# A streaming encoder step on one core: norm sums of the FFN as columns, the adds of the second half on VectorE, a new order of transfers before the down projection, and three low parts on GpSimd

## What is computed

```python
x = x + mixed @ w_out                       # three kinds of attention heads
x = x + memory_attend(x, mem_k, mem_v, ...) # cross-attention to 256 memory tokens, ends in @ w_mem_o
u = rmsnorm(x, g_ffn) @ w_up                # D_FF = 2816, so 5632 columns
c = causal depthwise convolution of width 3 over tokens of u
a, b = split(c); x = x + (silu(a) * b) @ w_down
y = rmsnorm(x, g_final)
```

## Time and profile before

| | |
|---|---|
| median of 3 runs | 1693.22 us (1693.13 to 1694.28) |
| the profiled execution | 1690.41 us, its span from the first to the last instruction 1688.6 us |
| PE busy | 1627.8 us (96%) |
| PEld busy | 1500.7 us (89%) |
| DVE busy | 1180.0 us (70%) |
| ACT busy | 674.3 us (40%) |
| POOL busy | 489.6 us (29%) |
| mean granted TensorE clock | 0.99 of full speed |

### The profile page before, as it was taken

How to read it: one execution, slowest core, us unless ns; L and a number is a source line. 1 busy time by engine, 2 the same in 40 slices (tenths; PEclk the granted TensorE clock), 3 DMA queues, 4 the chain that set the end, 5 groups by cost and what they waited for, 6 DMA issues and landing times.

```text
span 1688.6 us, 29368 instructions
## 1 busy us (share of the span) xinstructions
PE 1627.8 (96%) x11113; PEld 1500.7 (89%) x11113; DVE 1180.0 (70%) x1595; ACT 674.3 (40%) x1283; POOL 489.6 (29%) x255
## 2 busy tenths in 40 slices
PE   9999999999999999999967999999999998999998
PEld 8999889776667799998967999999999988999987
DVE  7583587896667654446698888888888855766765
ACT  7320222686566531215335555555555531011022
POOL 2683132000000223430564323333332222333432
PEclk9999999999999999999979999999999999999999
DMA  5322220330213223316521221222222144123213
GB/s 209 103 75 82 82 61 16 114 95 1 113 51 98 85 94 123 108 38 268 186 92 35 69 69 62 78 78 78 78 78 77 39 175 167 59 100 106 78 63 113
DMA packets 71236, 155.93 MB, mean 92 GB/s; under 512 B 29680, under 2 KB 32976, under 8 KB 68336
## 3 DMA queue, kind: packets, MB, share of 16 engines
q1 hardware_dynamic: 68848, 145.33, 25.3%
q10 hardware_dynamic: 2304, 9.44, 1.6%
HBM read 119.61 MB, written 32.86 MB: 90 GB/s over the span
## 4 chain that ended last, share of the span: by engine, by line
PE 86%; DVE 7%; issue 3%; ACT 2%; POOL 1%; DMA 1%; SPq 0%; DVEq 0%; ACTq 0%; POOLq 0%
PE scores L2644 20%; PE scores L3356 19%; PE bank L2644 17%; PE bank L3356 8%; PE scores L2950 3%; PE bank L3010 3%; PE bank L3034 2%; PE scores L2740 2%; PE scores L2662 1%; DVE x L2387 1%; DVE kbuf L2177 1%; PE bank L3304 1%; PE bank L2653 1%; PE scores L2973 1%; PE bank L3068 1%
## 5 line engine op out<-in xcount | busy, mean ns | idle before, releaser
L3356 PE MATMUL scores<-c,up_w 128*128 128x288 f32 x2464 | 365.7, 298 | 10.6 <-ACT kept_a L1735 3.7
L3356 PEld LDWEIGHTS scores<-c,up_w 128*128 128x128 f32 x2464 | 344.4, 190 | 13.0 <-issue 9.8
L1115 POOL TENSOR_TENSOR w_hi<-w_raw,zero 128x1024 fp32r<-128x1024 f32 x34 | 67.8, 1994 | 582.9 <-DVE prob L2193 262.2
L2644 PE MATMUL bank<-s_hi,w_down 128*128 128x384 f32 (+2 forms) x476 | 133.1, 339 | 8.2 <-POOL w_down L1253 5.5
L2644 PE MATMUL scores<-s_hi,w_down 128*128 128x384 f32 (+2 forms) x484 | 133.4, 336 | 0.0
L1850 ACT ACTIVATE s_hi<-s_raw 128x1152 fp32r<-128x1152 f32 x22 | 24.3, 1158 | 183.0 <-DMA s_raw<-s_mid 183.0
L2644 PEld LDWEIGHTS bank<-s_hi,w_down 128*128 128x128 f32 x476 | 87.9, 190 | 10.0 <-issue 8.9
L1250 POOL TENSOR_TENSOR w_down<-down_raw,zero 128x1024 fp32r<-128x1024 f32 x20 | 37.8, 1892 | 188.6 <-PE scores L2644 67.9
L1118 POOL TENSOR_TENSOR w_lo<-w_raw,w_hi 128x1024 fp32r<-128x1024 f32 x34 | 91.7, 2698 | 2.7
L2644 PEld LDWEIGHTS scores<-s_hi,w_down 128*128 128x128 f32 x484 | 88.7, 189 | 0.6
L2571 DVE TENSOR_TENSOR xd<-bank,xd 128x384 f32<-128x384 f32 x108 | 57.9, 551 | 39.0 <-PE bank L2644 39.0
(11 more groups left out here) (435 smaller groups left out, 4170.6 us busy)
## 6 DMA issues: line engine op xcount, KB each, us to landing
w_raw<-wstream SPq DMA_DIRECT2D x42, 512.0 KB, 3.6
s_raw<-s_mid SPq DMA_DIRECT2D x11, 1152.0 KB, 5.4
up_raw<-wstream SPq DMA_DIRECT2D x22, 512.0 KB, 4.2
x<-wstream SPq DMA_DIRECT2D x22, 512.0 KB, 4.4
s_mid<-conv SPq DMA_DIRECT2D x22, 512.0 KB, 2.8
down_raw<-wstream SPq DMA_DIRECT2D x22, 512.0 KB, 4.7
x_blk<-xT ACTq DMA_DIRECT2D x8, 576.0 KB, 4.7
x_mid<-x_blk ACTq DMA_DIRECT2D x8, 576.0 KB, 3.1
```

What stands on the lines that cost most here:

```text
L1115: pool.tensor_tensor(w_hi[:, k], w_raw[:, k], zero[:].unsqueeze(2).to_broadcast([P, KB, P]), ALU.add).then_inc(w_rounded, 1)
L2644: mm = pe.matmul(out, w[:, k, at + kb], x(kb), start=first and kb == 0 and n == 0, stop=last and kb == n_kb - 1 and n == 2)
L3356: mm = pe.matmul(bank[acc][:, 0:QF], up_w[i][:, w, tile(kb)], b[:, kb], start=i in (0, 1, 3) and kb == 0 and n == 0, stop=kb == 3 and n == ...
```

## The change

Five things, none of which changes what is computed:

1. Norm sums as columns. `half_sums(p)` now makes six matmuls of 96 tokens with `stat[p]` as the weights and a single column of ones, so that 96 partitions hold 6 sums each; the root and the reciprocal work on 96 x 6 values; `half_spread(p)` copies the result to all partitions in PSUM with six matmuls against the identity; `scale_rows` reads it from PSUM. The sums of half 0 follow piece 17 instead of 18, the scaling starts after piece 18 instead of 19.
2. The squares of half 1 are added on VectorE, between the residuals, instead of on GpSimd. `split_part(0, 5)` moves ahead into that loop.
3. ScalarE rounds the weights of slots `W_MO + 4` and `W_MO + 5` (`round_output_weights`); GpSimd only makes their low parts. ScalarE rounds weight 6 of unit 0 early, between squares 5 and 6 of half 0.
4. The low parts of inputs 4, 5 and 6 of half 1 are made on GpSimd, between two sums of unit 1's weights and the low parts of its first three, and signalled by `low_made`.
5. In the last unit product (0, half 1) goes between (4, half 0) and (5, half 0), and `hold(u, 1, 0)` goes ahead of `activate(u - 1)`. SP issues `store_s(NFF - 2)` first, two of the four `xd` loads after `load_s(1)`, and `load_down(2)`, `load_down(3)` ahead of `store_s(NFF - 1)`.

The core of the diff:

```diff
-MO_SUMS = 18
+MO_SUMS = 17
...
-SCALE_AFTER = {19: (0, 1), 20: (2, 3), 21: (4, 5), 22: (6, 7)}
-SPLIT_IN_MO = {23: 0, 25: 1, 27: 2, 29: 3, 30: 4}
-SUM_IN_MO = {24: (0, 1), 26: (2,), 28: (3,)}
+SCALE_AFTER = {18: (0, 1), 19: (2, 3), 20: (4, 5), 21: (6, 7)}
+ADD_AFTER = {20: 1, 22: 2, 24: 3, 26: 4, 28: 5, 30: 6}
+SPLIT_IN_MO = {22: 0, 23: 1, 26: 2, 29: 3, 30: 4, 31: 5}
+SUM_IN_MO = {24: (0,), 25: (1,), 27: (2,), 28: (3,)}
+FIRST_ORDER = [(i, p) for p in range(2) for i in range(7)]
+LAST_ORDER = [(i, 0) for i in range(5)] + [(0, 1), (5, 0), (6, 0)] + [(i, 1) for i in range(1, 7)]
+NF = 96
... SP
+            store_s(NFF - 2)
             sp.wait_ge(product, product_no(NFF - 1, 6, 0, True))
             load_s(0)
-            for n in range(4):
+            for n in range(2):
                 sp.dma_start(xd[:, 2 * n:2 * n + 2], io["x_mid"][:, 2 * n:2 * n + 2]).then_inc(x_in_again[n], 16)
-            store_s(NFF - 2)
             sp.wait_ge(product, product_no(NFF - 1, 1, 1, True))
             load_s(1)
+            for n in range(2, 4):
+                sp.dma_start(xd[:, 2 * n:2 * n + 2], io["x_mid"][:, 2 * n:2 * n + 2]).then_inc(x_in_again[n], 16)
+            load_down(2)
+            load_down(3)
             store_s(NFF - 1)
... GpSimd
             def split_again(slot):
-                pool.wait_ge(w_loaded[slot % 2], 8 * (slot - slot % 2) + 16)
-                pool.wait_ge(w_used, slot - 1)
-                split(slot % 2, slot - 1)
+                k = slot % 2
+                pool.wait_ge(w_rounded, slot - 1)
+                pool.tensor_tensor(w_lo[:, k], w_raw[:, k], w_hi[:, k].bitcast(F32), ALU.subtract).then_inc(w_split, 1)
...
+            pool.wait_ge(up_hi, 4)
+            pool.tensor_tensor(up_w[6][:, 1], up_source(0, 6), up_w[6][:, 0].bitcast(F32), ALU.subtract)
             split_again(W_MO + 4)
-            add_square(1)
-            add_square(2)
             split_again(W_MO + 5)
-            for j in range(3, KB):
-                add_square(j)
-            for i in range(3, 7):
-                up_low(0, i)
+            for i in range(3, 6):
...
             up_sum_3(1)
             up_sum_2(1)
+            def split_part(i):
+                pool.wait_ge(x_rounded, 2 * KB + 7 + i + 1)
+                pool.tensor_tensor(act_lo_of(i, 1), x_source(i, 1), act_hi_of(i, 1).bitcast(F32),
+                                   ALU.subtract).then_inc(low_made, 1)
+            split_part(4)
+            split_part(5)
+            split_part(6)
             for i in range(3):
                 up_low(1, i)
... ScalarE
+                act.wait_ge(sum_ready, Q_FFN + p + 1)
+                act.activation(half_root[0:NF, p], bank[6][0:NF, 0:6], ACT.Sqrt, bias=eps[0:NF],
+                               scale=1.0 / D).then_inc(sum_used, 1)
+            def round_output_weights(slot):
+                act.wait_ge(w_loaded[slot % 2], 8 * (slot - slot % 2) + 16)
+                act.wait_ge(w_used, slot - 1)
+                act.activation(w_hi[:, slot % 2], w_raw[:, slot % 2], ACT.Copy).then_inc(w_rounded, 1)
...
-            for j in range(4, KB):
+            for j in range(4, 6):
+                square_half(0, j)
+            round_up(0, 0, 0, 6)
+            for j in range(6, KB):
                 square_half(0, j)
             half_roots(0)
-            for j in range(3):
-                square_half(1, j)
+            square_half(1, 0)
+            round_output_weights(W_MO + 4)
+            square_half(1, 1)
             round_part(0, 0)
+            square_half(1, 2)
+            round_part(0, 1)
+            round_output_weights(W_MO + 5)
             square_half(1, 3)
-            round_part(0, 1)
...
             hold(u, 0, 0, True)
+            hold(u, 1, 0, True)
             activate(u - 1)
-            hold(u, 1, 0, True)
... VectorE
-                dve.reciprocal(stat[p][:, 1], stat[p][:, 1]).then_inc(rstd_ready, 1)
+                dve.reciprocal(half_root[0:NF, p], half_root[0:NF, p]).then_inc(rstd_ready, 1)
+            def scale_rows(p, rows):
+                dve.wait_ge(y_spread, p + 1)
...
+                    last = dve.scalar_tensor_tensor(row, row, const("g_ffn", m), spread_half, ALU.mult, ALU.mult)
...
-            for i in range(3, 7):
-                split_part(1, i)
+            split_part(1, 3)
... TensorE
+                for t in range(6):
+                    mm = pe.matmul(bank[6][0:NF, t:t + 1], stat[p][:, 0, NF * t:NF * t + NF], ones[:, 0:1], start=True,
+                                   stop=True)
+                mm.then_inc(sum_ready, 1)
+            def half_spread(p):
+                pe.wait_ge(rstd_ready, 3 + p)
+                for t in range(6):
+                    at = NF * (t % 3)
+                    mm = pe.matmul(bank[6 + t // 3][:, at:at + NF], half_root[0:NF, p, t:t + 1].to_broadcast([NF, P]),
+                                   ident[0:NF, 0:NF], start=True, stop=True)
+                mm.then_inc(y_spread, 1)
...
-            for p in range(2):
-                for i in range(7):
-                    up_product(0, i, p, True)
-                    if p == 0 and i == 1:
-                        half_sums(1)
+            for i, p in FIRST_ORDER:
+                up_product(0, i, p, True)
+                if (i, p) == (1, 0):
+                    half_sums(1)
+                if (i, p) == (2, 0):
+                    half_spread(1)
```

More of the change, by code:

```diff
@@ L198 @@
 N_G_DONE = 2 * (NZ + KB + GH) + N_MO - len(MO_LAST)
[L199 removed]
+Q_Y = Q_FFN + 2
+NF = 96
 def product_no(u, i, p, turned=False):
[L203 removed]
+    if not turned:
+        return N_PROD * u + 2 * i + p + 1
+    return N_PROD * u + (FIRST_ORDER if u == 0 else LAST_ORDER).index((i, p)) + 1
 def held_no(u, j, p, turned=False):
@@ L598, in build @@
         up_w[0:2] = [r(f"up_w{i}", [P, 2, 512], F32R) for i in range(2)]
-        stat = [Region(at_rstd + 6912 * (1 - p), 6912)(f"stat{p}", [P, 3, HF]) for p in range(2)]
+        stat = [Region(off_a if p == 0 else at_rstd, 6912)(f"stat{p}", [P, 3, HF]) for p in range(2)]
+        half_root = Region(at_rstd + 6912, 64)("half_root", [P, 2, 6])
         xd = Region(off_a, 8 * ROW)("xd", [P, KB, T])
@@ L621, in build @@
         bank = [S[i // 2][:, 512 * (i % 2):512 * (i % 2) + 512] for i in range(4)]
-        bank += [ctx.enter_context(nc.psum_tensor(f"bank{i}", [P, 512], F32))[:] for i in range(4, 8)]
+        bank += [ctx.enter_context(nc.psum_tensor(f"bank{i}", [P, 512], F32))[:] for i in range(4, 6)]
+        pair = ctx.enter_context(nc.psum_tensor("pair", [P, 1024], F32))
+        bank += [pair[:, 0:512], pair[:, 512:1024]]
+        spread_half = pair[:].rearrange("p (h n) -> p h n", h=2)[:, :, 0:QF]
         def const(name, k=0, n=1, rows=slice(0, P)):
@@ L1089, in _ @@
             for g in range(NGRP - 1):
-                for k in range(2):
-                    load_down(2 * g + 2 + k)
+                for d in range(2 * g + 2, 2 * g + 4):
+                    if d >= 4:
+                        load_down(d)
                 if g + 2 < NGRP - 1:
@@ L1794, in _ @@
             round_up(0, 0, 0, 5)
-            round_up(0, 0, 0, 6)
             half_roots(1)
@@ L3322, in half_sums @@
                 pe.wait_ge(x_summed, 2 * KB + 7 * p + 7)
-                for h in range(2):
-                    q = Q_FFN + 2 * p + h
-                    pe.wait_ge(sum_used, q - 1)
-                    pe.matmul(bank[6 + q % 2][:, 0:QF], ones[:], stat[p][:, 0, quarter(h)], start=True,
-                              stop=True).then_inc(sum_ready, 1)
+                if p:
+                    pe.wait_ge(b_made, 2)
+                for t in range(6):
[9 more added lines that the diff above has]
+                mm.then_inc(y_spread, 1)
             for d in range(MO_EARLY, N_MO):
@@ L3338, in up_product @@
                 if first:
-                    pe.wait_ge(x_split, 2 * KB + 7 * p + i + 1)
+                    if p and i >= 4:
+                        pe.wait_ge(low_made, i - 3)
+                    else:
+                        pe.wait_ge(x_split, 2 * KB + 7 * p + i + 1)
                 acc = (0, 2, 0, 4, 0, 0, 4)[i] + p
@@ L3374, in _ @@
                 unit(2 * i + 2)
-            for p in range(2):
-                for i in range(7):
-                    up_product(NFF - 1, i, p, True)
+            for i, p in LAST_ORDER:
+                up_product(NFF - 1, i, p, True)
             def down_projection(g, n):
                 first = isinstance(g, int) and g == 0
-                pe.wait_ge(x_split, N_PARTS + 2 * g + 2)
+                pe.wait_ge(x_split, N_PARTS - 3 + 2 * g + 2)
                 for m in range(KB):
```

60 lines of the change are left out of this document (26 added, 34 removed).

## The result

The changed kernel takes 1681.26 us in the median of 4 runs (1680.6 to 1683.26), the kernel before 1693.18 (4 runs, 1692.43 to 1694.28). The ratio is 0.9931, 95% interval 0.9914 to 0.9948: faster by 0.69%, 11.9 us by the medians, where 14.5 were forecast. The profiled execution took 1683.26, the slowest of the four, with a span of 1681.5; against the 1688.6 of before the spans differ by 7.1 only.

What follows compares the result with a forecast made beforehand. TensorE was taken as the bound, with gains only in its waits at two transitions: 14.0 us in the second plus 0.5 in the first, 14.5 from 1693.22, gives 1678.7 us (chance 0.51), range 1672.5 to 1687.5.

Steps and rivals of the forecast that it cites:

- the smaller one: First transition, memory output to up projection: 0.5 us gained in all, bounds -5.8 and +4.5.
- Second transition: Up projection to down projection, the larger term: TensorE's waits go, 14.0 us gained, lower bound 5.5.
- 3.4 before the down projection: Last unit's products: waits of 2.42 and one 0.59 go, with pipeline refill 3.4 us gained.
- 7.9 + 2.75: Start of the down projection: waits of 1.85 and 5.47 go, 7.9 us, and the 1.2 GHz level behind, 2.75.
- in part: Rival: second transition gained only in part because SP's queue holds up loads; gain 5.5 + 0.5, 1687.2 us, chance 0.12.
- Start of the first transition: Sums of half 0: TensorE waits 6 us instead of 1.54 since weight 6 is rounded early; 1.2 us lost.
- VectorE's list: VectorE's work from half 0's scaling to its last low part: 33.2 us instead of 35.4, ending at 873.3.
- hence scaling from 876.3 instead of 879.79: Norm of half 1: sums, root, reciprocal, product (2, 0) and spread run from 871, so scaling starts at 876.3.
- The low parts: Inputs 4 to 6 of half 1 on GpSimd, ahead of unit 1's weights: 2.69 us each, done at 904.7.
- the 5.3 of VectorE's lead: From the scaling of half 1 VectorE is 5.3 us ahead, shrinking to 0.3 at GpSimd's sum behind the low parts.
- slower through low parts: Rival: three low parts chained ahead of unit 1's weights cost more than the rest gives; at 9 us each 1697.6, chance 0.03.
- the first transition gets worse: Rival: low parts of 4 us, or a lowered clock slows pieces 18 to 21; gain 14.0 - 3.5, 1682.7 us, chance 0.17.

Runs made afterwards that it cites:

- e0: The changed kernel run again without edits, against the kernel before on the same chip: 1681.77 us, ratio 0.9935.
- e6: The kernel before with only the last unit's order of products and the hold ahead of the activation: 1690.68 us, ratio 0.9977.
- e7: The kernel before with only the new order of SyncE's transfers: 1683.50 us, ratio 0.9933 to the kernel before.
- e8: The changed kernel with 24 extra matmuls, results unread, ahead of the sums of half 1: 1678.98 us, ratio 0.9917 to the kernel before.
- e2: The changed kernel with the three low parts of half 1 back on VectorE: 1677.65 us, ratio 0.9913 to the kernel before.
- e4: The changed kernel with weight 6 rounded behind the last square of half 0 and the three low parts back on VectorE: 1675.15 us.
- e3: The changed kernel with weight 6 rounded behind the last square of half 0: 1678.06 us, ratio 0.9918 to the kernel before.
- e11: Same kernel as e4 but with the spread of half 1 right behind its sums, ahead of product (2, 0): 1676.65 us, ratio 0.9895.

## Why the prediction came out as it did

The 1678.7 and the sign were about right because its larger term was; the smaller one had the wrong sign in both profiles of the changed kernel, and both errors pull the same way: 14.5 forecast, 11.9 and 10.2 (e0) measured by medians. By the traces the two terms give 8.8 (13.0 - 4.3), so that the forecast stands only 2.6 from the measured median is in part luck.

**Second transition, 14.0 forecast, 13.0 in the traces.** Every wait that was to go went, for the reasons given: e6 and e7 take them away one part at a time. Of the 3.4 before the down projection 2.69 came. What was missed is the wait of 0.97 in place of 0.19: with TensorE earlier, VectorE's two low halves of the hidden rows are what it waits for, and they took 3.40 us, partly beside GpSimd's 2.40 on the down weights. 3.4 - 0.8 = 2.6. Of the 7.9 + 2.75 behind it 10.33 came, and the weights were not late: GpSimd waits for the twelfth piece, as said. The rival "in part" is out.

**Start of the first transition: right in kind.** A wait of 6 us was forecast, 6.46 came. The scaling of half 0 starts 1.95 us later than before, counted from the landing, 1.2 forecast. Root and reciprocal took 0.26 and 0.19 us (0.25 and 0.2 taken).

**VectorE's list: slightly off.** It ended at 874.59, 873.49 with the landing taken off, for 873.3. But the last add, forecast "near 871", ended when the sums of half 1 began, at 873.37: 872.3 with the landing taken off, 1.3 late.

**The step that failed is "hence scaling from 876.3 instead of 879.79".** It priced sums, root, reciprocal, product (2, 0) and spread at 5.3 us in sum, mostly at the 2.4 GHz level; at 1.2 GHz, after the 4.95 us wait in front of them, they took 7.71. e8 shows the same code in 4.44. (Within that sum, root and reciprocal were also too short: 2.6 us from the start of the sums to the end of the reciprocal for 1.85, with VectorE's copies ahead of it. Beside product (2, 0) this cost nothing.) With the 1.3 of the late add this is the whole 3.7 by which the scaling was later than said (881.08 - 1.10 = 879.98 for 876.3). The prediction counted such a loss behind the 5.47 wait of the second transition, and left the range 1.6 to 2.9 for the product (2, 0) alone; the same wait stood in the earlier trace rows at 873.14 with 5.13. A further 1.3 went at 0.50 too: ScalarE's first roundings of half 1 stand behind its copy of product (4, 0), done at 886.07 + 0.41, and VectorE waited 0.23 and 1.07 for them; in e8, at 1.00, these two waits are gone. So VectorE was not 5.3 ahead at the rounding of input 4 but 0.4 (901.41 - 1.10 for 900.74).

**The low parts: price right, place wrong.** 2.63 to 2.66 us each for 2.69. The Trainium skill's GPSIMD Engine Reference, section Engine selection, has GpSimd about twice as slow as VectorE with two inputs, an estimate of 2.7; the trace agrees. Three of them are 7.9 us ahead of unit 1's weights; the prediction let the 5.3 of VectorE's lead pay for them, and with a lead of 0.4 the sum behind them started 4.3 later (914.19 - 1.10 for 908.80) and the steady units 4.26 later. e2 takes them away and gets 6.2 back in stretch 2, e4 against e3 3.5. This is the mechanism of the rival "slower through low parts" at the normal price, and its size is that of the rival "the first transition gets worse" (-3.5 there, -4.3 here). The other half of that rival, memory output pieces so slow that VectorE meets them, is not in the two traces of the changed kernel, but it is in those of e4 and e11 (the wait of 1.46).

**Open.** The medians give the changed kernel 1.4 to 3.1 us more than its traces do (10.2 and 11.9 for 8.8 net of landing and tail). Both profiles of it are of its slowest executions, 1683.26 and 1683.15, and that of before is of a fast one; a clock that differs in the norms, as between e3 and e4, would do it, but the faster executions have no trace, so this isn't shown. Whether weight 6, late, pays in the time stays open too. Not tried: e4 with the matmuls of e8, which keeps product (2, 0) ahead of the spread.

## What to carry over

A lead that an engine gains can be spent only once it is there: before work is moved to an engine with a chain of its own (here 7.9 us in front of the next unit's weights), check that each link of the lead stands at the clock that the wait ahead of it leaves. A chain of tiny matmuls behind a wait of TensorE is to be priced at both levels: after waits of 4.94 and 4.95 us the sums ran at 1.2 GHz in all five traces that have them, after 3.41 and 3.53 once at 1.2 and once at 2.4. What one trace shows behind such a wait can be gone in the next, by 3 us here. And waits whose releasers are different queues are separate terms: in the second transition they could be added, and each of them checked with half of the change.
